# A two-part transformer kernel on one Trainium2 core: transposes of the activations move from stages of their own into the product that reads them

## What is computed

```python
for l in range(DEPTH):                      # part one, DEPTH = 2
    h = rms_norm(x, attn_norm[l])
    proj = h @ w_in[l]                      # then retention, sparse attention, gated mixing
    mix = jnp.concatenate([ret_o, nsa_o, gm_o], axis=-1)
    x = x + mix @ w_out[l]
    h = rms_norm(x, ffn_norm[l])
    gate, up = jnp.split(h @ w_gate_up[l], 2, axis=-1)
    x = x + (jax.nn.silu(gate) * up) @ w_down[l]
# part two: two more layers on 512 + 256 tokens, each a mixer (gated delta rule over
# 8 heads, then differential attention), an output product, a layer norm, a SwiGLU
# network and a layer norm; the input of each mixer and of each network is
# x * (1 + scale) + shift, with scale and shift computed from a condition vector
```

## Time and profile before

| | |
|---|---|
| median of 3 runs | 4373.13 us (4372.09 to 4377.51) |
| profiled execution | 4376.49 us, its span 4374.7 us |
| TensorE busy | 3815.9 us (87%) |
| VectorE busy | 2061.6 us (47%) |
| ScalarE busy | 868.6 us (20%) |
| GpSimd busy | 525.7 us (12%) |
| mean granted TensorE clock | 0.92 |

### The profile page before, as it was taken

The page is one execution under the profiler, slowest core; times in us unless marked ns, Lnnn a source line. Parts: engine busy times, 40 slices in busy tenths (PEclk is TensorE's granted clock), DMA queues, the critical chain, the costliest instruction groups (busy, mean ns, idle before and its releaser), DMA issues.

```text
span 4374.7 us, 50848 instructions
## 1 busy us (share of the span) xinstructions
PE 3815.9 (87%) x21060; PEld 3199.8 (73%) x21060; DVE 2061.6 (47%) x2818; ACT 868.6 (20%) x1516; POOL 525.7 (12%) x472
## 2 busy tenths in 40 slices
PE   4988899979888999689979898869999789967996
PEld 3776677757766777579968898658887668655885
DVE  3445333544353335565547454552224553755346
ACT  1114100211131002223422343010002111721012
POOL 1002000000010000105420452110000010520000
PEclk8878899988788999899989899979999889988998
DMA  3210244322103442210001002111111121002222
GB/s 121 80 56 1 113 173 173 116 78 77 49 7 127 173 173 106 81 39 11 1 17 48 11 1 102 48 45 62 68 58 68 68 75 58 11 31 75 97 91 83
DMA packets 48409, 314.07 MB, mean 72 GB/s; under 512 B 5772, under 2 KB 6540, under 8 KB 13752
## 3 DMA queue, kind: packets, MB, share of 16 engines
q1 hardware_dynamic: 37440, 272.65, 17.1%
q10 hardware_dynamic: 10744, 38.18, 2.4%
HBM read 301.25 MB, written 9.56 MB: 71 GB/s over the span
## 4 chain that ended last, share of the span: by engine, by line
PE 75%; DVE 9%; DMA 8%; POOL 3%; PEld 2%; ACT 1%; issue 1%; POOLq 1%; DVEq 0%; ACTq 0%; PEldq 0%; another core or an unknown queue 0%; SPq 0%
PE psum L505 18%; PE psum L506 17%; PE psum L507 17%; PE psum L1911 8%; DMA pieces_in<-pieces 6%; POOL xt_operands L659 2%; DVE pieces_lo L530 2%; PE psum L1909 2%; PE psum L1072 1%; PE psum L1045 1%; PE psum L862 1%; PE psum L2615 1%; PE psum L1056 1%; DVE x_mem L2100 1%; PE psum L2637 1%
## 5 line engine op out<-in xcount | busy, mean ns | idle before, releaser
L505 PE MATMUL psum<-xt_operands,pieces_hi 128*128 128x512 f32 (+1 forms) x2544 | 947.0, 372 | 82.9 <-DVE pieces_lo L530 80.5
L506 PE MATMUL psum<-xt_operands,pieces_hi 128*128 128x512 f32 (+1 forms) x2544 | 933.4, 367 | 0.0
L507 PE MATMUL psum<-xt_operands,pieces_lo 128*128 128x512 f32 (+1 forms) x2544 | 932.6, 367 | 0.0
L505 PEld LDWEIGHTS psum<-xt_operands,pieces_hi 128*128 128x128 f32 x2544 | 484.5, 190 | 204.3 <-DVE pieces_lo L530 110.0
L523 DVE CAST pieces_hi<-pieces_in 128x2048 fp32r<-128x2048 f32 x206 | 252.0, 1223 | 677.7 <-DMA pieces_in<-pieces 590.6
L506 PEld LDWEIGHTS psum<-xt_operands,pieces_hi 128*128 128x128 f32 x2544 | 484.4, 190 | 78.1 <-issue 2.6
L507 PEld LDWEIGHTS psum<-xt_operands,pieces_lo 128*128 128x128 f32 x2544 | 483.8, 190 | 78.5
L530 DVE TENSOR_TENSOR pieces_lo<-pieces_in,pieces_hi 128x2048 fp32r<-128x2048 f32 x206 | 471.9, 2291 | 5.7
L505 PE MATMUL psum<-pieces_hi,xt_operands 128*128 128x512 f32 (+1 forms) x1000 | 404.5, 405 | 79.0 <-DVE pieces_lo L530 72.2
L507 PE MATMUL psum<-pieces_hi,xt_operands 128*128 128x512 f32 (+1 forms) x1000 | 392.4, 392 | 0.0
L506 PE MATMUL psum<-pieces_lo,xt_operands 128*128 128x512 f32 (+1 forms) x1000 | 392.3, 392 | 0.0
(11 more groups left out here) (294 smaller groups left out, 4939.8 us busy)
## 6 DMA issues: line engine op xcount, KB each, us to landing
pieces_in<-pieces SPq DMA_DIRECT2D x260, 1024.0 KB, 4.8
arena<-mods ACTq DMA_DIRECT2D x8, 512.0 KB, 14.6
arena<-ln ACTq DMA_DIRECT2D x4, 1024.0 KB
x_park<-x_mem ACTq DMA_DIRECT2D x1, 3072.0 KB, 12.2
o_park<-arena ACTq DMA_DIRECT2D x2, 1536.0 KB
arena<-o_park ACTq DMA_DIRECT2D x1, 3072.0 KB
x_mem<-x_park ACTq DMA_DIRECT2D x1, 3072.0 KB, 19.0
arena<-line ACTq DMA_DIRECT2D x6, 448.0 KB, 5.8
```

The costliest lines, as they stand in the source:

```text
L505: signal_later(k, pe.matmul(out, sh, mh, start=start, stop=False))
L506: signal_later(k, pe.matmul(out, sh, ml, start=False, stop=False))
L507: return pe.matmul(out, sl, mh, start=False, stop=stop)
```

## The change

Eleven of the twelve transposing stages are gone from the lists. Their transposes are issued by TensorE inside the product's own function (class TurnPe), four PSUM banks ahead (three in ffn1). The twelfth, before the gates, remains a stage, with the new division of the evacuation. Two kinds of evacuation take the place of the old one:

- scaled (norm or plain copy): ScalarE writes the high part straight from PSUM, VectorE computes PSUM times scale minus high part in one operation.
- shifted (scale and shift): ScalarE writes the fp32 value, VectorE copies it to the high part and then subtracts.

GpSimd has no part in either. The RMS scaling is divided between ScalarE (tiles 0, 2) and VectorE (tiles 1, 3).

```diff
+class TurnPe:
+    def upto(self, count):
+        ahead = len(self.turn.banks)
+        while self.n < min(count, len(self.turn.jobs)):
+            kt, t0, m = self.turn.jobs[self.n]
+            if self.n >= ahead:
+                self.pe.wait_ge(self.released, self.n - ahead + 1)
+            for t in range(m):
+                last = self.pe.transpose(self.turn.bank(self.k, self.n)[:, t * P:(t + 1) * P],
+                                         self.src[:, t0 + t, kt * P:(kt + 1) * P], self.k.ident)
+            last.then_inc(self.k.S.tr_done, 1)
+            self.n += 1
+    def need(self, kt, t0):
+        n = self.turn.place[kt, t0]
+        self.upto(n + len(self.turn.banks))
+        self.pe.wait_ge(self.k.S.x_lo_ready, n + 1)
+def turn_scaled_act(k, e, dst, turn, scale=None):
+    for n, kt, t0, span in turn.each():
+        act.wait_ge(S.tr_done, n + 1)
+        act.activation(dst[0][:, kt, span], turn.bank(k, n), ACT.Copy,
+                       scale=scale(kt) if scale else 1.0).then_inc(S.x_hi_ready, 1)
+def turn_scaled_dve(k, e, dst, turn, scale=None, halfway=None):
+    for n, kt, t0, span in turn.each():
+        if halfway and n == len(turn.jobs) // 2:
+            halfway()
+        dve.wait_ge(S.x_hi_ready, n + 1)
+        if scale:
+            ins = dve.scalar_tensor_tensor(lo, turn.bank(k, n), scale(kt), hi, ALU.mult, ALU.subtract)
+        else:
+            ins = dve.tensor_tensor(lo, turn.bank(k, n), hi, ALU.subtract)
+        ins.then_inc(S.x_lo_ready, 1)
+def turn_shifted_dve(k, e, dst, turn):
+    for n, kt, t0, span in turn.each():
+        dve.wait_ge(S.tr_taken_act, n + 1)
+        dve.tensor_copy(dst[0][:, kt, span], k.value(dst[1][:, kt, span])).then_inc(S.x_hi_ready, 1)
+        if n:
+            rest(n - 1)
+    rest(len(turn.jobs) - 1)
...
 def in_t_dve(k, e, _):
-    for n in range(7):
+    split_dve(k, e, 0)
+    rms_dve(k, e, "attn_norm", IN_TURN)
+    for n in range(1, 7):
         split_dve(k, e, n)
...
 def rows_pe(k, e, slot, xT, nt, chunks, turn=None):
...
+                if turn and part == 0 and n == 4:
+                    turn.upto(len(turn.turn.jobs))
+                    pe.wait_ge(S.x_lo_ready, len(turn.turn.jobs))
                 for i in range(4):
+                    if turn and c == 0 and t % 4 == 0:
+                        turn.need(4 * part + i, t)
...
+def out_dve(k, e, _):
+    split_dve(k, e, 0)
+    turn_scaled_dve(k, e, (k.x1h, k.x1l), ROWS_TURN[NT1], halfway=lambda: split_dve(k, e, 1))
+    for n in range(2, 4):
         split_dve(k, e, n)
...
 def ffn_dve(k, e, silu, hid, hs, nt, finish, skipped=lambda f: 0, between=None, late=None, turn=None):
     split_dve(k, e, 0)
+    if turn:
+        turn()
...
 def dap_pe(k, e, slot, _):
+    turn = modt_turn_pe(k, pe, NT2)
     for n in range(16):
-        head_columns_pe(k, pe, slot, n, SEGS if n >= 8 else SEGS[:1])
-        if n >= 1:
+        head_columns_pe(k, pe, slot, n, SEGS if n >= 8 else SEGS[:1], turn)
+        if n == 1:
+            turn.upto(2 * KT)
+            pe.wait_ge(S.x_lo_ready, 2 * KT)
+        if n == 2:
+            da_rotate_pe(k, pe, 0)
+        if n >= 2:
             da_rotate_pe(k, pe, n - 1)
...
 def dap_act(k, e, _):
     act.dma_start(k.c3, T["c3"]).then_inc(S.loaded, 16)
+    gate_rows_act(k, e, 1)
+    modt_act(k, e, 1, 0, NT2)
     act.dma_start(k.rotary, T["rotary"]).then_inc(S.loaded, 16)
```

More of the change, by code:

```diff
@@ L653, in transposes_pool, with __init__, bank, each @@
-def transposes_pool(k, e, dst, nt):
-    for n, (kt, t0, m) in enumerate(tr_jobs(nt)):
-        span = slice(t0 * P, (t0 + m) * P)
-        e.eng.wait_ge(k.S.x_hi_ready, n + 1)
-        lo = dst[1][:, kt, span]
-        e.eng.tensor_tensor(lo, k.value(lo), dst[0][:, kt, span].bitcast(F32), ALU.subtract)
-def rms_pe(k, e, slot):
-    e.eng.wait_ge(k.S.normed_ready, NT1)
-    transposes_pe(k, e.eng, k.hn, NT1)
-def rms_act(k, e, name):
+class Turn:
+    def __init__(self, nt, banks=(4, 5, 6, 7), groups=(range(KT),)):
+        self.jobs = [(kt, t0, min(4, nt - t0)) for kts in groups for t0 in range(0, nt, 4) for kt in kts]
+        self.place = {job[0:2]: n for n, job in enumerate(self.jobs)}
+        self.banks = banks
+    def bank(self, k, n):
+        return k.ps[:, self.banks[n % len(self.banks)], 0:self.jobs[n][2] * P]
+    def each(self):
+        return [(n, kt, t0, slice(t0 * P, (t0 + m) * P)) for n, (kt, t0, m) in enumerate(self.jobs)]
@@ new lines, in turn_shifted_act, with rest @@
+def turn_shifted_act(k, e, dst, turn, scale, shift):
+    act, S = e.eng, k.S
+    for n, kt, t0, span in turn.each():
+        act.wait_ge(S.tr_done, n + 1)
+        act.activation(k.value(dst[1][:, kt, span]), turn.bank(k, n), ACT.Identity, bias=shift(kt, t0),
+                       scale=scale(kt, t0)).then_inc(S.tr_taken_act, 1)
+def turn_shifted_dve(k, e, dst, turn):
+    dve, S = e.eng, k.S
+    def rest(n):
+        _, kt, t0, span = turn.each()[n]
+        lo = dst[1][:, kt, span]
+        dve.wait_ge(S.x_hi_ready, n + 1)
+        dve.tensor_tensor(lo, k.value(lo), dst[0][:, kt, span].bitcast(F32), ALU.subtract).then_inc(S.x_lo_ready, 1)
+    for n, kt, t0, span in turn.each():
+        dve.wait_ge(S.tr_taken_act, n + 1)
[3 more added lines that the diff above has]
+    rest(len(turn.jobs) - 1)
@@ L669, in rms_act @@
+IN_TURN = Turn(NT1)
+FFN1_TURN = Turn(NT1, banks=(5, 6, 7))
+def rms_act(k, e, name, turn):
     act, S = e.eng, k.S
@@ L699, in in_t_pe @@
         for kt in range(KT):
+            if g == 0:
+                turn.need(kt, 0)
             at = (g % 2) * 1024 + kt * P
@@ L1197, in rows_pe @@
         for part in range(2):
+            if turn and c == 0 and part == 1:
+                turn.upto(len(turn.turn.jobs))
             w = take_split(k, pe, slot, 2 * c + part)
@@ L1232, in add_dve, with ffn_pe @@
         dve.tensor_tensor(xs, k.ps[:, bank_of(n), :], xs, ALU.add).then_inc(S.mm_taken, 1)
-def ffn_pe(k, e, slot, xT, hs, nt, between=None, late=None):
+def ffn_pe(k, e, slot, xT, hs, nt, between=None, late=None, turn=None):
     pe, S = e.eng, k.S
@@ L1246, in ffn_pe @@
             for kt in range(KT):
+                if turn and f == 0 and half == 0:
+                    turn.need(kt, 0)
                 c = 1024 * half + kt * P
@@ L1294, in ffn_act, with ffn_dve @@
                        ACT.Copy).then_inc(S.hs_hi_ready, 1)
-def ffn_dve(k, e, silu, hid, hs, nt, finish, skipped=lambda f: 0, between=None, late=None):
+def ffn_dve(k, e, silu, hid, hs, nt, finish, skipped=lambda f: 0, between=None, late=None, turn=None):
     dve, S = e.eng, k.S
@@ L1387, in ffn1_pe @@
     last.then_inc(S.ada_begun, 1)
-    ffn_pe(k, e, slot, k.both(NT1), k.hs, NT1, between, late)
+    pe.wait_ge(S.normed_ready, NT1)
+    turn = TurnPe(k, pe, k.hn, FFN1_TURN, S.x_lo_ready)
+    turn.upto(3)
+    ffn_pe(k, e, slot, k.both(NT1), k.hs, NT1, between, late, turn)
 def cond_act(k, e, _):
@@ L1674, in head_columns_pe @@
         for kt in range(KT):
+            if turn and n == 0:
+                turn.need(kt, at // P)
             col = 256 * kt + P * (n % 2)
@@ L2426, in ffn_all_pe @@
                 for kt in range(KT):
+                    if f == 0 and half == 0:
+                        turn.need(kt, at // P)
                     c = 1024 * half + kt * P
@@ L2570, in dap_dve @@
     dve, S = e.eng, k.S
-    for n in range(2):
-        split_dve(k, e, n)
+    split_dve(k, e, 0)
+    modt_dve(k, e, NT2)
+    split_dve(k, e, 1)
     dve.wait_ge(S.lam_loaded, 32)
```

217 lines of the change are left out of this document (91 added, 126 removed).

## The result

The changed kernel takes **4236.19 us** (median of 4 runs, 4231.27 to 4240.71), the kernel before, run beside it, 4375.01 (4372.09 to 4377.51): ratio 0.9683, 95% interval 0.9666 to 0.9699, 139 us less. The forecast was 4246, the range 4212 to 4290.

What follows compares the result with a forecast made beforehand. It took the time as TensorE's work plus its idle stretches around transposes; eight terms summed to 127.2 us, from the profiled 4376.5 to 4249.3, and with the median 3.4 us lower, 4246 us; range 4212 to 4290.

Steps and rivals of the forecast that it cites:

- item 2: ffn1 (two turns): 18.9 us gained for both, after 4.2 us charged each for VectorE waiting for a weight piece.
- 0.50 beyond the first 6 us of a turn: Sign that would prove the prediction wrong: the clock still at half (0.50) after a turn's first 6 us.
- the first rival: Clock stays at 1.2 GHz through each turn's first group, 24 matmuls slower: 54 us lost, 4300 us; chance 0.10.
- Common terms: Scaled turns: +1.8 us from clock and fewer transposes, -1.6 us per 512-token turn for just-in-time waits at 0.1 us each.
- items 1 and 3: Two input products of part one, 26.4 us gained (13.2 each); three output products for 512 tokens, 34.3 us.
- Item 4: Output product for 768 tokens: 11.6 us gained, with TensorE 2.8 us idle at token tile 4.
- Item 5: ffn_all: VectorE sets the pace, at 1.18 then 0.78 us a job; 20.4 us instead of 34.0, 13.6 gained.
- Item 6: dap: head tile 2 starts at 27.0 us instead of 36.4, behind ScalarE's rotary table load; 9.4 us gained.
- Item 8: The remaining transposing stage: 16.5 us on VectorE instead of 18.2, 1.7 us gained.
- Items 3 and 7: Three output products for 512 tokens, 34.3 us gained; last network, 14.3 us instead of 25.6, 11.3 gained.
- The clock, row against rule: A profile row shows transposes reaching full clock; a skill page says they do not, which would give 4266 us.
- the +1.8 us: Gain per scaled turn: three matmuls at half clock instead of eight, and some nine transposes fewer.

Runs made afterwards that it cites:

- rows_spread: Changed kernel with the 768-token output product's transposes of jobs 4 to 15 spread between matmuls and VectorE's second split behind its turn: 4226.47 us, 0.9661.
- dap_gates: Changed kernel with ScalarE's four gate-row DMAs in dap issued behind the turn, not ahead of it: 4238.08 us, 0.9686.
- dap_both: dap_gates plus TensorE issuing dap's last transposes behind head tile 0, not head tile 1: 4227.47 us, 0.9655.
- the control: The changed kernel run a second time with no edit: 4238.08 us, 0.9684 against the kernel before.

## Why the prediction was right, and where it was not

The mechanism held in the main: the wait around the transposes went, the transposes stayed, and no rival's time came true. In eight of the eleven turns the first split began 1.1 to 1.2 us after the stage, so its piece was there; in layer two's input turn it began after 5.0 us but was done 8.0 us before the first transpose; in ffn1 it began after 4.4 and 4.5 us, which is item 2. In all the splits waited 506.7 us, less than the 590.6 of the earlier trace rows.

One sign that the prediction had named against itself did show: "0.50 beyond the first 6 us of a turn". In the first turn the clock is up after 4.0 us, but in four of the eleven, the first output turn, ffn_all, dap and the last output turn, it came up only after 8.4, 8.5, 12.1 and 9.2 us. This is dap, from 6 to 12 us behind its first transpose:

```profile
3389.85:3395.85 6.00, 5.96 (x19) 4.81 (x20) 3.30 (x8) 1.73 (x3) 0.00 (x0) 0.50 0.53 193
```

TensorE was busy through it and the clock stayed down, so the first rival was there in part, for nine product matmuls at most and not for 24. The sum was 12 us short, and by its terms:

- **Common terms, the 0.1 us for each just-in-time wait (items 1 and 3).** The lower bound, nothing, was right: one k-tile follows the other every 1.13 us (65.35, 66.48, 67.61 in the timeline), 0.67 for its matmuls and 0.46 for its transposes, where 0.55 + 0.2 stood in the sum. Eight times 0.29 is 2.3 us, about the 2.4 that each input turn gave beyond 13.2; the output turns gave 1.2 to 1.6 more.
- **Item 2, VectorE's wait for the weight piece.** 4.2 us were charged. The split was done at 454.9 us and the squares at 453.1, so VectorE was 1.8 us late, and 1.1 of that lay beside ScalarE's load of a table of 1.28 us, which it begins without VectorE. The squares themselves came 1.0 us later behind ScalarE's own DMA issues, and the divided scaling gave 0.6 back. The first transpose came 11.65 us after the output product instead of 10.5, 1.1 later and not 2.6 to 5.8. The contention that was feared did not show: the piece, requested at 446.4, let VectorE go at 451.4, after 5.0 us. (Its price does not follow from its own figures either: 1.75 MB at 2.5 us each are 4.4 us, not 3.2, and no run here shows the 2.5.)
- **Item 4.** The 2.8 us idle were 4.2, but the term left out what an idle TensorE costs behind it: half clock for some 9 us more. Run rows_spread gives that back.
- **Item 5** has the right number by a wrong step, which is luck. After the first product matmul VectorE does not set the pace; TensorE waited for it 0.30 us once and 0.07 once. The k-tile takes TensorE 1.12 us, which happens to be VectorE's 1.18.
- **Item 6 failed as a mechanism.** Head tile 2 was to start 27.0 us in, behind the rotary table and ScalarE. It started at 30.5 behind VectorE's second split, which itself waited for transposes that TensorE only issued behind head tile 1, after gate-row issues had held ScalarE's first evacuation back (6.04 us in the window above). I had the right queue of work, but put the end of head tile 1 at 20 us instead of 22.8 and the split one step too early. At head tile 2 the stage was still 7.3 us ahead of the kernel before, by its end 3.4. Of the 4.0 lost in between, 2.6 are thirteen matmuls at half clock behind that wait; one rotation that had moved behind head tile 2 is under 1 us more. Runs dap_gates and dap_both show both causes.
- **Item 8.** VectorE's pair was priced at the sum of two durations and a gap, 1.18. In the trace the records overlap, and a pair follows the other every 0.94 us (0.54 for 256 columns). Sixteen pairs make 3.8 us, and the term missed by 3.1.
- **Items 3 and 7** were right within 4 and 0.2 us, item 7 by luck: its turn gave 12.8 us, 1.5 more than forecast, and the clock took 1.6 back behind the later pause.

**The clock, row against rule.** The rule that transposes do not bring full clock would have given 4266; the result is 30 us under it. That alone decides little, since the waits costed at 18 us cost nothing. The counts, from the clock records of the traces, decide: before, 93 matmuls ran at half clock at the start of the eleven products, 8.5 on average; in the changed kernel it is 35 and in the control 39, 3.2 and 3.5 on average (none to nine in a turn), where the +1.8 us assumed three instead of eight. And in the kernel before, in eleven of the twelve transposing stages, the clock came up or came back to 1.00 between 3.2 and 5.8 us after the first transpose, with nothing but transposes on TensorE.

**What I had not asked** was which half of the change pays. Its headline, transposes inside the product, is worth 24 us on top of the rest; the evacuation without GpSimd, the joined stages and the split ahead give the other 115. The order matters: the overlap with the old evacuation takes 80 us and the new evacuation without the overlap 115, each with joined stages and the split ahead. Much of that they share, so their gains do not add; added last, the new evacuation is worth 59.

Open: no run joins the stages without the new evacuation. The division of the first 79 us, some 69 for the evacuation and 13 for the joining, is read from windows of two executions, and the divided scaling and ffn1's earlier raw pieces are in neither figure.

## What to carry to other kernels

Before an operation is interleaved, take out its waits: short jobs on engines that do not hold each other up, stages joined, and the next stage's first split pulled ahead gave nearly five times what the overlap then added. Where work is interleaved, look at what each queue holds behind the last interleaved jobs: waits of 4.2 and 6.2 us there cost TensorE another 4.4 and 2.6 us in clock. And price a pipelined pair by the distance between starts, not by the sum of its durations.
